# Two norms in a row taken from one input, and one head's centring moved ahead of the next head's values

## The reference

```python
def rms_norm(x, g):
    return x * rsqrt(mean(x * x, axis=-1) + EPS) * g

def mlstm_mixer(...):                      # 4 heads of 128 channels
    ...
    mu = mean(h, axis=-1)
    var = mean(square(h - mu), axis=-1)
    hn = (h - mu) * rsqrt(var + EPS) * norm_g
    return sigmoid(o_pre) * hn

def second_block(x, ...):
    ...
    x = x + gt2 * (square(relu(h @ w_mlp1)) @ w_mlp2)
    return rms_norm(x, g_final)            # the stream that goes on

def third_block(x, ...):
    h = rms_norm(x, norm1_w) * (1.0 + scale1) + shift1
    p = h @ w_in
    ...
    x = x + gate1 * (merged @ w_out)       # the normalized stream is used here, much later
```

## Time and profile before

| | |
|---|---|
| median of 3 runs | 3603.9 us (3601.74 to 3605.94) |
| the profiled execution | 3597.89 us, of which the span of the trace is 3596.1 us |
| PE busy | 96% of the span |
| DVE, ACT, POOL busy | 56%, 39%, 20% |
| mean granted clock of PE | 0.975 of full speed |
| last result of `mlp_phase`'s PE units to the first matmul of `front_phase` | 2491.5 to 2514.9 us of the span |
| `mlstm_phase` | 1592 to 1752 us of the span |

### The profile page before, as it was taken

One profiled execution on the slowest core, in us unless ns is written; L12 is line 12 of the kernel. 1 busy time (PEld: TensorE's weight loads), 2 busy tenths in 40 slices (PEclk: granted clock), 3 DMA queues, 4 the chain that ended last, 5 costly groups with the idle time before them and its releaser, 6 DMA issues. The chain is left out here.

```text
span 3596.1 us, 59385 instructions
## 1 busy us (share of the span) xinstructions
PE 3442.4 (96%) x25339; PEld 2623.7 (73%) x25339; DVE 2011.9 (56%) x3150; ACT 1411.5 (39%) x2335; POOL 733.6 (20%) x379
## 2 busy tenths in 40 slices
PE   8999999997999999999999999998998999999998
PEld 5778888886644447676777778886768887878887
DVE  4138888886399984743444555333675534265422
ACT  4247777774201114442444443223444224233322
POOL 0000000001200000223222344443620002434442
PEclk9999999998999999999999999999999989999999
DMA  7722222224455652413211333331311103323332
GB/s 267 248 67 63 57 62 79 57 57 119 122 186 184 188 186 74 119 30 77 54 48 47 88 94 104 96 100 43 98 39 50 27 3 89 95 81 100 94 92 72
DMA packets 519915, 337.83 MB, mean 94 GB/s; under 512 B 31739, under 2 KB 494132, under 8 KB 519140
## 3 DMA queue, kind: packets, MB, share of 16 engines
q1 hardware_dynamic: 519652, 334.04, 31.9%
HBM read 321.39 MB, written 12.62 MB: 93 GB/s over the span
## 5 line engine op out<-in xcount | busy, mean ns | idle before, releaser
L1587 DVE SCALAR_TENSOR_TENSOR conv_u<-cv_pad,vec,conv_u 128x512 f32<-128x512 f32 (+1 forms) x540 | 327.1, 682 | 0.0
L4024 POOL TENSOR_TENSOR tl_wl<-tl_w,tl_wh 128x1024 fp32r<-128x1024 f32 (+1 forms) x103 | 244.3, 2372 | 356.2 <-ACT tl_wh L4144 356.2
L1410 PE MATMUL cv_bank<-hT,cv_w 128*128 128x512 f32 x704 | 313.8, 599 | 0.0
L1410 PEld LDWEIGHTS cv_bank<-hT,cv_w 128*128 128x128 f32 x704 | 130.1, 190 | 163.8 <-issue 163.8
L4144 ACT ACTIVATE tl_wh<-tl_w 128x1024 fp32r<-128x1024 f32 (+1 forms) x103 | 107.5, 1043 | 329.8 <-PE tl_bank L4062 329.8
L2714 POOL TENSOR_TENSOR mp_wl<-mp_w,mp_wh 128x1024 fp32r<-128x1024 f32 x72 | 173.2, 2408 | 221.2 <-ACT mp_wh L2801 215.1
L738 PE MATMUL hg_bank<-hg_hh,hg_wh 128*128 128x512 f32 x512 | 210.3, 411 | 4.6 <-PEq L202 4.6
L740 PE MATMUL hg_bank<-hg_hh,hg_wl 128*128 128x512 f32 x512 | 203.1, 397 | 0.0
L739 PE MATMUL hg_bank<-hg_hl,hg_wh 128*128 128x512 f32 x512 | 202.6, 396 | 0.0
L4060 PE MATMUL tl_bank<-tl_room,tl_wh 128*128 128x512 f32 x464 | 183.8, 396 | 4.2 <-DVE tl_room L4285 3.3
L4062 PE MATMUL tl_bank<-tl_room,tl_wl 128*128 128x512 f32 x464 | 182.5, 393 | 0.0
(11 more groups left out here) (839 smaller groups left out, 8897.9 us busy)
## 6 DMA issues: line engine op xcount, KB each, us to landing
cv_ada<-in_w_ada_dram SPq DMA_DIRECT2D x48, 1024.0 KB, 7.7
hg_w<-in_hgrn_w_in_dram SPq DMA_DIRECT2D x64, 512.0 KB, 7.0
mp_w<-in_w_mlp_dram SPq DMA_DIRECT2D x64, 512.0 KB, 4.0
open_w<-in_ada_w_dram SPq DMA_DIRECT2D x12, 2048.0 KB, 10.4
cv_w<-in_conv_w_in_dram SPq DMA_DIRECT2D x44, 512.0 KB, 4.2
tl_w<-in_w_ffn_in_dram SPq DMA_DIRECT2D x44, 512.0 KB, 3.8
side_w<-in_w_in_dram SPq DMA_DIRECT2D x24, 512.0 KB, 4.1
fr_w<-in_w_in_dram SPq DMA_DIRECT2D x24, 512.0 KB, 3.8
```

Source lines behind the costliest of these rows:

```text
L1410: ins = pe.matmul(ps[n % RING][:, :], slot(n)[:, k * P:(k + 1) * P], K.hT[:, k, :], start=(k == 0), stop=(k == KD - 1))
L1587: ins = dve.scalar_tensor_tensor(o, x, by, o, ALU.mult, ALU.add)
L4024: pool.tensor_tensor(WL[u % SPLIT][:, 0:n, :], W[u % RAW][:, 0:n, :], WH[u % SPLIT][:, 0:n, :].bitcast(F32), ALU.subtract).then_inc(low, 1)
```

## The change

It has two parts.

**The seam.** `accumulate(1, i)` now makes two sums on DVE: `both`, the sum of the squares weighted by g² + EPS (new; in the buffer `mp_t`), and after it `mp_acc` as before. PE multiplies `both` with ones (one matmul in place of the eight of L2788), then `mp_acc`. ACT takes the root of `both` first (into `K.root3`, with EPS² as bias), then `root(1)` (into `mp_rstd`, now also `K.root2`). ACT's eight squares and DVE's eight scalings of the stream between the two roots are gone from `mlp_phase`. The scalings stand in `front_phase`, one behind the weighted sum of each of the first eight units, in place, with `K.root2`. `front_phase` scales the unnormalized stream by `K.gain3`, which has the final norm's gain in it and is made in `mlp_phase`, before the first `residual_add`, by five small operations together with the weights `G`, in place of L3336.

**The mLSTM.** `centres(s - 2)` on PE and `centred(s - 2)` on DVE are issued before `values(s - 1)`; `variances` and `rooted` stay behind it. ACT's stream is not touched.

```diff
@@ mlstm_phase, PE @@
                 for s in range(MH):
                     weights(s)
+                    if s >= 2:
+                        centres(s - 2)
                     if s >= 1:
                         values(s - 1)
                     if s >= 2:
-                        centres(s - 2)
                         variances(s - 2)
                 turns()
+                centres(MH - 2)
                 values(MH - 1)
-                centres(MH - 2)
                 windows()
@@ mlstm_phase, DVE @@
                     weights(s)
+                    if s >= 2:
+                        centred(s - 2)
                     if s >= 1:
                         values(s - 1)
                     if s >= 2:
-                        centred(s - 2)
                         rooted(s - 2)
...
+                centred(MH - 2)
                 values(MH - 1)
...
-                centred(MH - 2)
                 rooted(MH - 2)
@@ mlp_phase @@
-        rstd = K.sb(st, "mp_rstd", [P, T])
+        rstd = K.root2 = K.sb(st, "mp_rstd", [P, T])
+        K.gain3 = K.sb(st, "mp_gain3", [P, KD])
+        G = K.sb(st, "mp_weight", [P, KD])
+        eps2 = K.sb(st, "mp_eps2", [P, 1])
+        both = t[:, 0, :]
@@ mlp_phase, PE @@
+                pe.wait_ge(both_ok, KD)
+                pe.matmul(SUM[0][:, :], K.ones[:, :], both, start=True, stop=True).then_inc(x_sum, 1)
                 squares(1)
-                for k in range(KD):
-                    pe.wait_ge(x_sq, k + 1)
-                    pe.matmul(SUM[0][:, :], K.ones[:, :], sq[:, k % 2, :], start=(k == 0), stop=(k == KD - 1)).then_inc(x_sum, 1)
@@ mlp_phase, ACT @@
-                root(1)
-                for k in range(KD):
-                    act.wait_ge(normed, k + 1)
-                    if k >= 2:
-                        act.wait_ge(x_sum, k - 1)
-                    act.activation(sq[:, k % 2, :], K.xT[:, k, :], ACT.Square).then_inc(x_sq, 1)
-                act.wait_ge(x_sum, KD)
-                act.activation(K.root3[:, :], SUM[0][:, :], ACT.Ln, scale=1.0 / DM, bias=K.epsc[:, 0:1]).then_inc(x_ln, 1)
+                act.wait_ge(x_sum, 1)
+                act.wait_ge(weighted, 5)
+                act.activation(K.root3[:, :], SUM[0][:, :], ACT.Ln, scale=1.0 / DM, bias=eps2[:, 0:1]).then_inc(x_ln, 1)
                 act.wait_ge(x_ln, 1)
                 act.activation(K.root3[:, :], K.root3[:, :], ACT.Exp, scale=-0.5).then_inc(x_ln, 1)
+                root(1)
@@ mlp_phase, DVE: accumulate @@
                     dve.wait_ge(squared, KD * n + i + 1)
+                    if n == 1:
+                        if i == 0:
+                            dve.tensor_scalar(both, acc[:, :], G[:, 0:1], None, ALU.mult).then_inc(both_ok, 1)
+                        else:
+                            dve.wait_ge(both_ok, i)
+                            dve.scalar_tensor_tensor(both, sq[:, i % 2, :], G[:, i:i + 1], both, ALU.mult, ALU.add).then_inc(both_ok, 1)
@@ mlp_phase, DVE: before the first residual_add @@
+                dve.tensor_tensor(G[:, :], K.vec[:, gf:gf + KD], K.vec[:, gf:gf + KD], ALU.mult).then_inc(weighted, 1)
+                dve.memset(eps2[:, :], EPS * EPS).then_inc(weighted, 1)
+                dve.scalar_tensor_tensor(K.gain3[:, :], K.mod[:, scale3:scale3 + KD, 3], 1.0, K.vec[:, g3:g3 + KD], ALU.add, ALU.mult).then_inc(weighted, 1)
+                dve.wait_ge(weighted, 3)
+                dve.tensor_scalar(G[:, :], G[:, :], EPS, None, ALU.add).then_inc(weighted, 1)
+                dve.tensor_tensor(K.gain3[:, :], K.gain3[:, :], K.vec[:, gf:gf + KD], ALU.mult).then_inc(weighted, 1)
@@ mlp_phase, DVE: the end @@
                 accumulate(1, KD - 1)
-                dve.wait_ge(rstd_ok, 2)
-                for k in range(KD):
-                    dve.scalar_tensor_tensor(K.xT[:, k, :], K.xT[:, k, :], K.vec[:, gf + k:gf + k + 1], rstd[:, :],
-                                             ALU.mult, ALU.mult).then_inc(normed, 1)
@@ front_phase, DVE @@
-                dve.scalar_tensor_tensor(gain[:, :], K.mod[:, SCALE:SCALE + KD, v], 1.0, K.vec[:, g1:g1 + KD], ALU.add, ALU.mult).then_inc(gained, 1)
-                dve.wait_ge(gained, 3)
                 scaled(0)
...
                     dve.scalar_tensor_tensor(pb[:, i, :], diff[:, p, :], K.vec[:, mu + i:mu + i + 1], pad[:, p, 3:3 + T],
                                              ALU.mult, ALU.add).then_inc(shifted, 1)
+                    if i < KD:
+                        dve.scalar_tensor_tensor(K.xT[:, i, :], K.xT[:, i, :], K.vec[:, gf + i:gf + i + 1], K.root2[:, :],
+                                                 ALU.mult, ALU.mult).then_inc(gained, 1)
```

More of the change, by code:

```diff
@@ L2666, in mlp_phase @@
         (high, low, summed, relu_ok, res_ok, g_high, g_low, squared, sq_sum, ln_ok, rstd_ok, gained, t_ok, h_high, h_low,
-         d_high, d_sq, d_low, normed, up_sum, opened, closed, added, merged_ok, acc_ok, x_sq, x_sum, x_ln) = sems[RAW:RAW + 28]
+         d_high, d_sq, d_low, weighted, up_sum, opened, closed, added, merged_ok, acc_ok, both_ok, x_sum, x_ln) = sems[RAW:RAW + 28]
         y_high, y_low, bw_high, bw_low = sems[32:36]
@@ L2913, in accumulate @@
                     dve.wait_ge(squared, KD * n + i + 1)
+                    if n == 1:
[4 more added lines that the diff above has]
+                            dve.scalar_tensor_tensor(both, sq[:, i % 2, :], G[:, i:i + 1], both, ALU.mult, ALU.add).then_inc(both_ok, 1)
                     if i == 0:
+                        if n == 1:
+                            dve.wait_ge(both_ok, 1)
                         dve.sem_inc(acc_ok, 1)
@@ L2963, in _ @@
                 dve.scalar_tensor_tensor(gain[:, :], K.mod[:, SCALE:SCALE + KD, v], 1.0, K.vec[:, g2:g2 + KD], ALU.add, ALU.mult).then_inc(gained, 1)
+                g3, scale3 = K.at["g1_3"], M3 + 8
+                dve.tensor_tensor(G[:, :], K.vec[:, gf:gf + KD], K.vec[:, gf:gf + KD], ALU.mult).then_inc(weighted, 1)
[4 more added lines that the diff above has]
+                dve.tensor_tensor(K.gain3[:, :], K.gain3[:, :], K.vec[:, gf:gf + KD], ALU.mult).then_inc(weighted, 1)
                 for u in range(KD):
@@ L3081, in front_phase @@
         diff = K.sb(st, "fr_diff", [P, 2, T])
-        rstd = K.root3
-        gain = K.sb(st, "fr_gain", [P, KD])
+        rstd, gain, gf = K.root3, K.gain3, K.at["final_2"]
         r1 = K.sb(st, "fr_rows", [P, T])
```

## The result

| | before | after |
|---|---|---|
| median of 20 runs each, us | 3604.32 | 3620.97 |
| lowest to highest, us | 3600.31 to 3606.81 | 3588.52 to 3624.92 |
| profiled execution, us (span) | 3597.89 (3596.1) | 3618.86 (3617.1) |
| its mean granted clock | 0.975 | 0.967 |

The ratio of after to before is 1.0031, with a 95% interval of 1.0017 to 1.0045. The forecast was 3592.5 us in a range of 3586.5 to 3598.0, faster; it was wrong in size and in sign. What the median hides is that the changed kernel has two times. Of its 20 runs, four took 3588.5, 3590.4, 3591.7 and 3599.6 us, at a mean clock of 0.974 to 0.976, three of them within the forecast's range; the other sixteen took 3617.5 to 3624.9 us, at 0.966 to 0.968. The profile is of one of the sixteen.

The account below looks back on a forecast made before the run. PE, busy 96% of the span, was taken as the bound, so only its waits or removed work give time. Seam 11.4 us, scalings and mLSTM 0: 3603.9 - 11.4 = 3592.5 us, range 3586.5 to 3598.0.

Parts of the forecast that it names:

- Rival 3: PE's restart behind the seam: clock stays at half rate for five units, losing 17.6 us, 3610.1 us; chance 0.02.
- nothing up to T = 9: PE's restart behind the seam: a slow stretch of T us costs nothing up to T = 9.
- The formula: PE's restart behind the seam: a slow stretch of T us costs 0.44 T - 2.5 - 1.5.
- Seam 11.4 us: End of `mlp_phase` into `front_phase`: phase ends 11.37 us earlier, plus 0.1 for the gain, rounded down to 11.4.
- PE's first pair: Seam: PE's first short sum over channels after the last `residual_add`, taken as 1.12 us.
- Scalings 0: `front_phase`: eight scalings, 6 us on DVE, fit into 1.9 us free per unit, so cost 0.
- small operations 0: Before the first `residual_add`: five small operations need 0.9 us, covered by 1.47 us of idle DVE, so cost nothing.
- rival 2: `front_phase`: each scaling on DVE blocked to 2.86 us and 7.4 us of lag reach PE, 3599.9 us; chance 0.07.
- mLSTM 0: mLSTM: the moved centring gains 0, as ACT's square waits for its own order and the `side_w` transfer.
- bounds +5.4 and -0.3: mLSTM: gain of at most 5.4 us if both waits went, loss of 0.3 us if ACT's copy were late.
- Rival 1: mLSTM: PE's waits ahead of `variances` go too, 5.4 us more gained, 3587.1 us; chance 0.05.
- I would be wrong if the restart runs for more than 9 us at 0.50: Sign against the forecast: PE's restart behind the seam staying at the 1.2 GHz clock level for over 9 us.

Follow-up runs that it names:

- e16_seam_burst_24: Seam part alone (mLSTM order as before) plus three full matmuls in level 1 and 24 single ones in levels 4 and 5; 3590.47 us.
- e17_before_burst_24: Kernel before plus three useless full matmuls in level 1 and 24 single ones in levels 4 and 5; 3598.4 us.
- e13_seam_one_burst: Seam part alone (mLSTM order as before) plus one burst of three useless full matmuls in level 1; 3596.46 us.
- e14_before_one_burst: Kernel before plus one burst of three useless full matmuls in level 1; 3604.15 us.
- e2_mlstm_only: Kernel before with only the mLSTM's new order, without the seam part; 3605.72 us, ratio 1.0004.
- e9: Whole change plus five bursts of three useless full matmuls, one in level 1 and four in levels 4 and 5; 3601.21 us.
- e11: Seam part alone (mLSTM order as before) plus five bursts of three useless full matmuls in levels 1, 4 and 5; 3598.93 us.
- e12: Whole change plus one burst of three useless full matmuls in level 1; 3596.70 us.
- e18: Whole change plus three useless full matmuls in level 1 and 24 single ones in levels 4 and 5; 3591.63 us.
- e3_change_14: Whole change plus 14 useless chained squares on ACT at the end of `mlp_phase`, as idle time put back; 3603.39 us.

## Why the prediction was wrong

**The step that failed is one that it did not write down**: that whatever stands behind `front_phase` shifts by 11.4 us and keeps its length, a term put at nothing without a reason. The runs showed in its place that the levels, 390 us behind, took 28.6 us longer, with the clock low for 102 us instead of 34. Rival 3 named the right mechanism, a clock that stays low, and the right price: 0.44 us for each us at half rate, from the earlier trace rows, against some 30 us for 68 us in the levels. But it looked for it at one place only, the restart behind the seam, and gave it 0.02. There the clock was low from 2501 to 2508 and from 2518 to 2522 us (2511 to 2521 before), and of the 9.7 us gained at the first matmul 8.3 were left at the copies. From the restart on that is some 6 us at half rate in either kernel, where "nothing up to T = 9" was said. The formula took the slow time as hidden behind PE's waits for DVE; the second stretch came behind the last of them (1.97 us, at 2517.91), and 3.4 x 0.44 = 1.5 us is the estimate for it, near the 1.4 lost. The profile before had the warning in plain sight: the 8 in the clock line at the levels. A stretch of 34 us at half rate, which no line of the program asks for, was already costing 34 x 0.44 = 15 us, and nothing said that its length was fixed. If it began at the start of the levels and lasted to their end it would eat the gain and more, and that case belonged among the rivals, with a chance well above 0.02.

Point by point, for the rest:
- *Seam 11.4 us.* 10.5 by the trace; the term that was mis-sized is PE's first pair, at half clock (2.07 us for 1.12). In `e16_seam_burst_24`, where it ran at full clock, the seam is 6.76 us long, for 6.94 forecast. In the medians of the kernels it is 7.7 and 7.9 us. The two profiles in which the clock did the same in the levels (low for 3 us in the first, `e17_before_burst_24` and `e16_seam_burst_24`) have the levels start 10.8 us apart, end 10.7 apart, and the last instruction 11.0: nearly the forecast, where nothing else moves. Some of the difference to the medians are the 1.4 us in `front_phase`; another part may be the low stretch around level 1 (10 us long in the profile of `e13_seam_one_burst`, 3 in that of `e14_before_one_burst`, so 3 us by the same price). That is one profile each, and argued rather than shown.
- *Scalings 0, small operations 0.* Right; rival 2 fell.
- *mLSTM 0, bounds +5.4 and -0.3.* Rival 1 fell: the square follows the rounded weight. The bound on the side of the loss (0.3) may have been too narrow. `e2_mlstm_only` is 2.1 us above before, within the noise (0.9996 to 1.0013), and the medians of the pairs with and without the moved centring differ by 2.3 (`e9`, `e11`), 0.2 (`e12`, `e13`) and 1.2 us (`e18`, `e16`; the last two pairs across series). All have the sign of a loss, but the runs of each pair overlap. In the profiles the phase, from the first matmul of L2100 to the last of `mixes` (L2158 before), takes 151.4 to 157.0 us in the old order (12 profiles, mean 154.9) and 155.0 to 157.0 in the new (8, mean 156.3). The clock accounts for that: within the phase it was low for 21.6 us on average in the old order and 24.7 in the new, and 3.1 x 0.44 = 1.4 us. So the order costs between 0 and 2 us, and apart from the clock the phase is as long as before, as forecast. Whether the new order makes the clock fall more often or these 20 profiles only happen to show it so, is open.
- *"I would be wrong if the restart runs for more than 9 us at 0.50".* From its first matmul on it ran at 0.50 for 3 and again for 3 us, and the forecast was wrong all the same: the sign that I had named covered only the place I was looking at.

**What is shown and what is open.** Shown: the loss is in the clock of the levels (profile, and the mean clock of every run, 0.967 for 0.975; these 0.008 are some 58 us more at half rate over the span, the 68 of the levels less some 11 elsewhere). It is not in the work that the change added: idle time removes it (`e3_change_14`), it occurs in before, and with three more matmuls no run has it (`e12_change_one_burst`, across series). Open: why the clock, once it has fallen in the first level, rises after 3 us in one kernel and after 102 in another, when the instructions there are the same, and what part the chip has in how often. The Trainium skill ("TensorE: Matmul & The Clock Gate", "Seeing it yourself") tells of a gate that stays low for over 50 us. That was at a quarter of the rate, and the level here is a half. The prediction found no such row in this case; the 102 us after are the nearest to one, and the experiments say that both the moment (`e3_change_14`) and what PE is given in the meantime (`e12_change_one_burst`, `e16_seam_burst_24`) bear on how long it lasts.

## What to carry to other kernels

Before forecasting an edit, list every stretch in which the granted clock is low, also far from the edit and also if its engine is called busy, and ask for each what happens if it starts earlier or lasts. When a kernel turns slower although the edited place got faster, subtract the starts of the same lines through the rest of the trace, and test the suspicion by putting idle time back: a kernel that gets faster by idling has told you that its cause is a matter of when, not of what. Look at all run times and their mean clocks, not at a median; two groups of runs 30 us apart mean that a few full matmuls at the right place may be worth more than the edit.

## What the runs showed of the hardware that I had not expected

- TensorE at half rate while it is busy without a gap. In the window of 2936 to 2971 before, PE is busy for 35.00 of 35.00 us and the clock stands at 0.52; after, it stays low for 102 us over some 1800 matmuls, nearly all small. In every profile it has risen within 6 us of the last matmul of the levels.
- Three full matmuls (0.62 us) among 128 of 64x64 weights and 32 columns: in the seven profiles that have them and the shortened seam, the clock either does not fall there or is up again after 3 to 10 us; in the two that have the seam and no added matmul or idle time, it stays at 1.2 GHz for 102 us. 40 single ones spread over the levels left the long fall in 3 and 2 of 12 runs (116 us in the profile of one), 56 in 1 of 12. In levels 4 and 5, 16 did not hold the clock and 24 did.
- A single full matmul between groups of 64x64 tiles costs 0.42 us, near four times its 256 columns at full rate (0.11 us); three together cost about 0.6 (2890.70 and 2891.24 in `e12_change_one_burst`).
- The same program, on the same chip, has the long fall in one run and not in the next: 16 of 20 runs after, 6 of 12 with the seam alone, 2 of 11 of before with 3.3 us of idling, 4 of 32 of before in one series. In the other series, on other chips, before had it in none of 20, 35, 32, 28 and 16 runs.
